# A residual stack in four layers: each step from layer to layer done by token halves

## The reference

```
layer 0: h = rms_norm(x); proj = h @ even_w_in (1024 -> 5120)
         stick-breaking attention (8 heads of 128), a diagonal state-space mixer with GLU
         x = x + concat(o_a, o_b) @ even_w_out            (1536 -> 1024)
layer 1: h = rms_norm(x); proj = h @ odd_w_in (1024 -> 3088)
         gated linear attention (4 heads, chunks of 64)
         x = x + (o * silu(z)) @ odd_w_out                (1024 -> 1024)
layers 2, 3: mod = silu(c) @ w_ada + b_ada -> shift, scale, gate
         h = rmsnorm(x, norm_w) * (1 + scale) + shift
         qa ka va za qr kr vr zr ga gr = h @ w_in         (1024 -> 11264)
         dilated window attention on qa ka va, retention on qr kr vr
         merged = sigmoid(ga) * (y_att @ w_proj_attn) + sigmoid(gr) * (y_ret @ w_proj_ret)
         x = x + gate * (merged @ w_out)
output:  rmsnorm(x, final_norm_w)
```

## Time and profile before

| | us |
|---|---|
| median of 3 runs | 1103.94 |
| the profiled execution, its own time | 1104.06 |
| its span | 1101.1 |
| TensorE busy | 1027.7 (93%) |
| VectorE busy | 706.2 (64%) |
| ScalarE busy | 554.3 (50%) |
| GpSimd busy | 319.2 (29%) |
| TensorE's share of the chain that ended last | 84% |
| VectorE's share of that chain | 9% |

### The profile page before, as it was taken

How to read it: one execution, slowest core, us unless ns; L and a number is a source line. 1 busy time by engine, 2 the same in 40 slices (tenths; PEclk the granted TensorE clock), 3 DMA queues, 4 the chain that set the end, 5 groups by cost and what they waited for, 6 DMA issues and landing times.

```text
span 1101.1 us, 15234 instructions
## 1 busy us (share of the span) xinstructions
PE 1027.7 (93%) x6032; PEld 901.5 (82%) x6032; DVE 706.2 (64%) x1043; ACT 554.3 (50%) x822; POOL 319.2 (29%) x342
## 2 busy tenths in 40 slices
PE   5899999978998799999999989969999999999994
PEld 5688888767976699888899868858998888988883
DVE  6884857568759664556566686676454565758664
ACT  6978577447334354455443334434444555334442
POOL 3600150016323534371708750045150000420001
PEclk9899999989999899999999999989999999999997
DMA  7543424467745676774667655546676436654541
GB/s 236 167 117 100 149 77 145 145 187 253 230 141 179 211 218 205 231 218 141 194 190 220 194 180 174 190 134 205 188 232 188 135 115 176 189 151 148 181 152 57
DMA packets 94470, 191.10 MB, mean 174 GB/s; under 512 B 6800, under 2 KB 10128, under 8 KB 94400
## 3 DMA queue, kind: packets, MB, share of 16 engines
q1 hardware_dynamic: 86256, 164.71, 48.9%
q0 software_dynamic: 6992, 22.72, 6.8%
q10 hardware_dynamic: 1152, 2.71, 0.7%
HBM read 189.07 MB, written 1.05 MB: 173 GB/s over the span
## 4 chain that ended last, share of the span: by engine, by line
PE 84%; DVE 9%; ACT 4%; issue 1%; DMA 1%; DVEq 0%; SPq 0%; ACTq 0%
PE G L579 15%; PE G L581 15%; PE G L580 15%; PE G L588 8%; PE G L590 8%; PE G L591 8%; DVE WL L1494 2%; PE B L542 2%; ACT AR L1039 1%; ACT WH L1039 1%; PE B L675 1%; DVE AR L1594 1%; PE G L615 1%; PE G L614 1%; PE G L613 1%
## 5 line engine op out<-in xcount | busy, mean ns | idle before, releaser
L1494 DVE TENSOR_TENSOR WL<-RAW,WH 128x1024 fp32r<-128x1024 f32 (+2 forms) x306 | 393.9, 1289 | 292.0 <-ACT WH L1039 291.1
L1039 ACT ACTIVATE WH<-RAW 128x1024 fp32r<-128x1024 f32 (+2 forms) x306 | 320.4, 1049 | 297.0 <-PE G L581 168.5
L579 PE MATMUL G<-WH,HTh 128*128 128x512 f32 (+2 forms) x624 | 252.1, 404 | 8.6 <-DVE WL L1494 8.4
L581 PE MATMUL G<-WL,HTh 128*128 128x512 f32 (+2 forms) x624 | 241.5, 387 | 0.0
L580 PE MATMUL G<-WH,HTl 128*128 128x512 f32 (+2 forms) x624 | 241.3, 387 | 0.0
L588 PE MATMUL G<-HTh,WH 128*128 128x256 f32 x736 | 211.4, 287 | 4.9 <-DVE HTl L1599 4.1
L590 PE MATMUL G<-HTl,WH 128*128 128x256 f32 x736 | 208.9, 284 | 0.0
L591 PE MATMUL G<-HTh,WL 128*128 128x256 f32 x736 | 208.8, 284 | 0.0
L588 PEld LDWEIGHTS G<-HTh,WH 128*128 128x128 f32 x736 | 141.9, 193 | 8.3 <-issue 6.9
L579 PEld LDWEIGHTS G<-WH,HTh 128*128 128x128 f32 x624 | 118.4, 190 | 33.8 <-DVE WL L1494 11.1
L590 PEld LDWEIGHTS G<-HTl,WH 128*128 128x128 f32 x736 | 141.9, 193 | 0.6 <-issue 0.5
(11 more groups left out here) (346 smaller groups left out, 1240.2 us busy)
## 6 DMA issues: line engine op xcount, KB each, us to landing
RAW<-in_w_in SPq DMA_DIRECT2D x176, 512.0 KB, 3.8
RAW<-in_even_w_in SPq DMA_DIRECT2D x40, 512.0 KB, 3.6
AR<-in_w_ada POOLq DMA_DIRECT2D x80, 256.0 KB, 3.5
RAW<-in_odd_w_in SPq DMA_DIRECT2D x16, 512.0 KB, 4.5
RAW<-in_w_proj_ret SPq DMA_DIRECT2D x16, 512.0 KB, 3.4
RAW<-in_w_out SPq DMA_DIRECT2D x16, 512.0 KB, 3.5
RAW<-in_even_w_out SPq DMA_DIRECT2D x12, 512.0 KB, 3.5
AR<-in_w_ada SPq DMA_DIRECT2D x16, 256.0 KB, 4.3
```

What stands on the lines that cost most here:

```text
L579: nc.tensor.matmul(o, xh, wh, start=begins, stop=False)
L581: ins = nc.tensor.matmul(o, xh, wl, start=False, stop=ends)
L1039: return nc.scalar.activation(out_, ps, ACT.Copy, **kw)
L1494: vt(wl, raw, wh.bitcast(F32), ALU.subtract).then_inc(*dve.mark(LO, n))
```

## The change

Every step from layer to layer is now done first for tokens 0-127 and then for tokens 128-255:

- The last three pieces of a layer are of kind C, instead of the last two: column half 0 with the last rows, column half 1 with the rows before the last, column half 1 with the last rows. All three run for tile 0, then all three for tile 1 (`split_half`).
- The first three pieces of layers 1, 2 and 3 are done the same way (`opening`): three half steps for tile 0, three for tile 1. They are of kind N, which a split needs; in layers 2 and 3 the `va` groups therefore move ahead of `qa` and `ka`.
- `rstd`, `scaled`, `square` and `turned` work on one tile each. VectorE scales columns 0-511 of a tile and GpSimd columns 512-1023 (before: VectorE and ScalarE). The turned blocks are evicted in runs of 128x128; in layers 2 and 3 ScalarE applies shift and scale (before: VectorE).
- `hi` of the new layer's first piece moves behind the first squares; the tables of ScalarE and VectorE end 6 half steps before a layer's end instead of 4.
- HN32 now lies on OR. GpSimd's modulation tasks of layers 2 and 3 each wait for a piece to be read (`pool.wait_ge(*read(time // 2 - 1))`) and have new places in the table. At the start of layer 1 three DMAs of GpSimd stand behind its two scalings.
- The first norm (layer 0) is also done by tiles on VectorE and GpSimd, and its transposes in the order column half 0 for both tiles, column half 1 for both.

The first `next_layer` below is ScalarE's, the second VectorE's, and `scaled` is GpSimd's:

```diff
-AT_ADA1 = tuple(2 + 30 * g + 3 * k + (36 if g > 5 else 0) for g in range(8) for k in range(8))
+AT_ADA1 = tuple(8 + 29 * g + 3 * k + (0, 20, 50)[g // 2 - 1 if g > 3 else 0] for g in range(8) for k in range(8))
...
+        def closing(l, w, ks, lhs, into):
+            v = w.rearrange("(c p) n -> p c n", p=P)
+            groups["close", l] = dict(into=into, at=len(pieces), n=512)
+            for j, k in ((0, ks[1]), (1, ks[0]), (1, ks[1])):
...
+        def opening(name):
+            for i in range(3):
+                pieces[groups[name]["at"] + i]["split"] = i
...
-                if p["kind"] == "C":
-                    closing_half(n, kk, p)
+                if p["split"] is not None:
+                    h = 2 * p["split"] + kk
+                    split_half(n - p["split"] + h % 3, h // 3)
...
+            def open_layer(l, first):
+                for q in range(2):
+                    norm_turn(l, 0, q)
+                for i in range(6):
+                    half(first + i)
+                    if i in (1, 2):
+                        norm_turn(l, 1, i - 1)
...
+            def next_layer(l):
+                square(l - 1, 0, 0)
+                square(l - 1, 0, 1)
+                hi(n0)
+                square(l - 1, 1, 0)
+                hi(n0 + 1)
+                turned(l, 0, 0)
+                square(l - 1, 1, 1)
+                turned(l, 0, 1)
+                hi(n0 + 2)
+                turned(l, 0, 2)
+                turned(l, 0, 3)
+                for r in range(4):
+                    turned(l, 1, r)
...
+            def next_layer(l):
+                residual(l - 1, 0, 0)
+                residual(l - 1, 0, 1)
+                residual(l - 1, 1, 0)
+                rstd(l, 0)
+                scaled(l, 0)
+                residual(l - 1, 1, 1)
+                lo(n0)
+                turned(l, 0, 0)
+                turned(l, 0, 1)
+                lo(n0 + 1)
+                rstd(l, 1)
+                scaled(l, 1)
+                lo(n0 + 2)
+                turned(l, 0, 2)
+                turned(l, 0, 3)
+                for r in range(4):
+                    turned(l, 1, r)
...
+            def scaled(l, ti):
+                pool.wait_ge(*RSTD.of(l, ti))
+                gts(HN[:, ti, 512:1024], X[:, ti, 512:1024], NR[l][:, ti:ti + 1], 0.0, ALU.mult, ALU.add).then_inc(
+                    *pool.mark(HN_P, l, ti))
...
             for l in range(2):
-                norm(2 + l)
+                next_layer(2 + l)
                 ts(GNH[l], co[f"gn{l}"], 0.5, None, ALU.mult).then_inc(*dve.mark(GNH_V, l))
...
+                        pool.wait_ge(*read(time // 2 - 1))
```

More of the change, by code:

```diff
@@ L1033, in gbank @@
             return G[groups[name]["into"][ti]]
-        ENDS = {2 * last_of(n) + 1: n for n in groups if n[0] not in ("o0c", "close")}
+        ENDS = {2 * last_of(n) + 1: n for n in groups if n != "o0c" and n[0] != "close"}
         def scalar_program():
@@ L1350, in scalar_program @@
             nc.scalar.activation(er, er, ACT.Exp).then_inc(*act.mark(S5_A, "er"))
-            for time in range(2 * groups["zr"]["at"] - 4):
+            for time in range(2 * groups["zr"]["at"] - 6):
                 if time in ENDS:
@@ L1400, in scalar_program @@
                     hi((time + 1) // 2 + AHEAD)
-            for ti in range(2):
-                squares(0, ti)
-            norm(1)
-            for time in range(2 * groups["zr"]["at"], 2 * H0[0] - 4):
+            next_layer(1)
+            for time in range(2 * groups["zr"]["at"], 2 * H0[0] - 6):
                 if time in ENDS:
@@ L2096, in residual @@
-            def residual(l):
-                for ti in range(2):
-                    dve.wait_ge(*tile(("close", l), ti))
-                    for n in range(2):
-                        ps = G[groups[("o0a", "o0b")[n] if l == 0 else ("o1", n)]["into"][ti]]
-                        x = X[:, ti, 512 * n:512 * n + 512]
-                        vt(x, ps[:, :], x, ALU.add).then_inc(*dve.mark(RES_V, l, ti, n))
-            nc.vector.memset(M3[:, :, :, :].rearrange("p a b c -> p (a b c)"), 0.0).then_inc(*dve.mark(S5_V, "zero"))
@@ L2164, in vector_program @@
                     lo((time + 1) // 2 + AHEAD)
-            residual(0)
-            norm(1)
+            next_layer(1)
             ts(go, co["gla_o_g"], 0.5, None, ALU.mult).then_inc(*dve.mark(GO, "g"))
-            for time in range(2 * groups["zr"]["at"], 2 * H0[0] - 4):
+            for time in range(2 * groups["zr"]["at"], 2 * H0[0] - 6):
                 if time in ENDS:
@@ L2366, in pool_program @@
             nc.gpsimd.memset(flat(NEAR), 0.0).then_inc(*pool.mark(S5_P, "near"))
[L2368 removed]
+            for ti in range(2):
+                scaled(0, ti)
+            for time in range(2 * groups["zr"]["at"] - 6):
                 if time == AT_S5["powers"]:
@@ L2378, in pool_program @@
             ada_load(0, 0)
-            pool.wait_ge(*read(53))
+            for ti in range(2):
+                scaled(1, ti)
             nc.gpsimd.dma_start(GM, const("glamask")).then_inc(l_gm, 16)
```

375 lines of the change are left out of this document (186 added, 189 removed).

## The result

The changed kernel took 1093.45 us (median of four runs, 1090.39 to 1093.97) against 1103.01 for the kernel before in the same comparison (four runs): ratio 0.991, 95% interval 0.988 to 0.994. That is 9.6 us faster, inside the forecast range and 1.7 us under the forecast. The profiled execution took 1093.02, its span 1091.2. The two profiled executions lie 11.0 us apart, their spans 9.9; the other 1.1 is outside the spans (2.96 us before, 1.8 after) and is not the change, since most later executions of the kernel before have 1.8 to 2.0 there too.

The account below looks back on a forecast made before the run. TensorE, busy 93% of the span, was taken as the bound, gaining only where it stands or runs slowly. Terms -0.6 - 4.7 - 7.4 - 1.6 + 2.3 + 3.1 = -8.9 gave 1095.2, median 1095.1 us; range 1089.5 to 1101.5.

Parts of the forecast that it names:

- The chains between the layers: From each layer's last matmul to the next layer's fourth piece: 0.6, 4.7 and 7.4 us gained at the three boundaries.
- T: End of a layer's last closing matmul (its start plus 0.39 us), from which the prediction counts times.
- Layer 1 to 2: Boundary between these layers: fourth piece at T+17.2 instead of T+21.87, 4.7 us gained.
- Layer 2 to 3: Boundary between these layers: fourth piece at T+18.35 instead of T+25.75, 7.4 us gained.
- the 1.0 that I put on tile 0's root beside GpSimd's add: Layer 2 to 3: GpSimd's add for tile 1 holds the port, so tile 0's rsqrt ends 1.0 us later.
- The end: Behind the last matmul: 2.1 us of work and waiting falls away, final weights' DMA takes 0.5 back, 1.6 gained.
- The start: Program's start: rsqrt chains one behind the other, VectorE waiting for GpSimd's memset, first matmul at 18.5, 2.3 us lost.
- The clock in the openings: Openings of layers 1 to 3: half steps two to four at 1.2 GHz, 3.1 us lost together.
- The GpSimd rival: Modulation tasks hold the port through layer 2's attention and retention; six more tasks lose 12 us, result 1107; chance 0.06.
- the four places of the change: The three layer boundaries and the program's end: gains of 0.6, 4.7, 7.4 and 1.6 us.
- losses of 5.4: Losses in the sum: 2.3 us at the program's start and 3.1 for TensorE's low clock in the openings.

Follow-up runs that it names:

- Closing whole: Changed kernel with each layer's last three pieces multiplied piece by piece, both token halves within each, instead of all three for tokens 0-127 first: 1102.1 us, ratio 0.998.
- scale_first: Changed kernel with GpSimd's clearing of buffers at the start put behind its scaling of tile 0 (the 128x2048 one behind both tiles): 1093.06 us, ratio 0.9915.
- mod_early: Changed kernel with the fifth group of GpSimd's eight modulation tasks 20 steps earlier in layer 2, out of the retention: 1090.6 us, ratio 0.9875.
- mod_around: Changed kernel with layer 2's fifth group of modulation tasks laid around the retention, four before and four after, the sixth group at steps 182-203: 1090.52 us, ratio 0.9887.
- fw_early: Changed kernel with the final norm's weights loaded in layer 3 and the first final product ahead of tile 1's reciprocal root: 1090.48 us, ratio 0.9884.
- order_only: Kernel before with only the piece order in layers 2 and 3 changed, attention's values first, then queries and keys: 1104.21 us, ratio 1.0001.

## Why the prediction was right, and where it was not

- **The chains between the layers: right in kind; in the sizes two errors cancelled.** Forecast fourth pieces T+14.75, T+17.2, T+18.35; measured T+14.35, T+18.10, T+18.46. First half step of layer 2 T+3.0, measured T+3.3. Transposes in groups of 8, 4, 4 with a first gap of 0.7, as forecast. Undoing either split showed that it is this chain and no side effect; how much of the split opening's part is the clock is not separated.
  - *Layer 1 to 2, 0.9 too much.* VectorE was on time: its scaling of tile 1 ended at T+8.6 for T+8.5. But GpSimd's, counted at 0.70, took 2.04 beside VectorE's `lo`, and VectorE's eviction behind the `lo` took 0.83 where 0.42 was counted, and where all others of its kind here measure 0.41 to 0.43; it ended 0.27 behind GpSimd's scaling:

```profile
376.55 2.04 POOL L2363 TENSOR_SCALAR TK<-X,SM 128x512 f32<-128x512 f32 x1 [7.00 <-DVE SM L1598]
```

```profile
378.02 0.83 DVE L1618 TENSOR_TENSOR HTl<-AR,HTh 128x256 fp32r<-128x256 f32 x1
```

  TensorE's third half step waited for that eviction and came at T+10.66 for T+10.1; everything of tile 1 stands behind it. GpSimd's columns themselves were not waited for: their transposes ran at 380.46, 1.9 us after its scaling. The other 0.3 is small excess behind the last eviction (T+15.6 for T+15.0): the group-norm instruction and a `lo` of 1.23.
  - *Layer 2 to 3, right by luck.* It has the same 0.9, and yet came only 0.1 late, since the 1.0 that I put on tile 0's root beside GpSimd's add was too much. The add ran from T-1.9 to T-0.6, and of the root's instructions beside it one took 0.47 instead of 0.22; VectorE's scaling ended 0.36 later than in layer 1 to 2, not 1.0, and the fourth piece came those 0.36 later, T+18.46 for T+18.10.
- **The end: near in size, on the wrong path.** 2.2 for 1.6. I followed VectorE's last product, and it ends at T+8.5 for T+9.4 before, 0.9 earlier and not 1.6. The span's end comes 7.6 us behind GpSimd's last product in every profile, and that one moved by 2.2, from T+8.85 to T+6.64: it no longer stands behind the root of both tiles, only behind the final weights. Closing whole confirms it: GpSimd's product ends at T+9.34 there, 2.7 later, as does the span.
- **The start: the step that failed.** I had the first tiny instruction of tile 0's root wait for GpSimd's clearing, since it took 2.42 us before. After:

```profile
6.08 0.15 DVE L1579 TENSOR_SCALAR SM<-SM 128x1 f32<-128x1 f32 x1 [0.94 <-ACT AR L1387]
...
8.07 2.59 DVE L1603 TENSOR_SCALAR TK<-X,SM 128x512 f32<-128x512 f32 x1
```

  The whole root ran beside the clearing, at 0.15 to 0.22 us an instruction; only the 128x512 scaling waited. The first matmul came at 16.17, not 18.5, and the term of 2.3 us measured 0.0 at T of layer 0. The instruction that waited before was 128x2, one column for each tile; now it is 128x1. The Trainium skill (VectorE: DVE Perf Modes, "Mode 2×_2P — use both read ports for one tensor") gives both read ports to a one-source operation from SBUF to SBUF whose outermost non-unit dimension is even, or odd and equal in source and destination, and (SBUF — State Buffer, "Who interferes with whom") has such an operation blocked by GpSimd. By that rule 128x2 and 128x512 wait; 128x1, which has no such dimension, doesn't. The traces agree in all three: 2.42, 2.59 and 0.15 us. No run here has the old 128x2 root in the new order, so the width as the cause rests on these rows and the rule. And `scale_first` showed that even a start 2.3 us earlier is worth nothing.
- **The clock in the openings: the term was of the wrong kind.** It stayed at 1.00 from 1 to 2 and fell at 0 to 1 and 2 to 3, but in the half steps that wait for VectorE anyway. The fourth piece of 2 to 3 came at T+18.46 with the clock at 0.60 in 732 to 736, and at T+18.49 in `mod_early` with no fall there. Where the fall reaches the dense half steps of tile 1 it costs about 1 us: T+15.37 for T+14.35 in `mod_around`, T+19.0 for T+18.1 in `mod_around` and `fw_early`. The 3.1 should have been 0 to 1 for each boundary, by where the fall lies, and in the forecast's sum it measured 0.
- **Inside the layers: a rival in part.** The GpSimd rival (tasks that hold VectorE up in the retention) was priced at 12 us for six more tasks; I had named it and then put nothing into the sum. What came is 2.6 us in layer 2, and it isn't more waiting: the longest wait grew from 2.05 to 3.38, but all waits of TensorE over 0.25 us behind the fourth piece sum to 4.5 before, 4.2 after and 3.0 in `mod_early`. What differs is the clock behind the wait, 0.50 from 649.9 to 656.7 and 1.00 throughout before. Moving the tasks took 2.4 us away in the profile, half of it waits. The +1.1 in layer 1 is not the change: the same 2.50 us wait stands in both kernels, and the clock behind it stayed up in the profile before and fell in the one after. `order_only`, whose layer 1 is the one of before, has the fall too. The stretches 268 to 272 of before, after and `order_only`:

```profile
268.00:272.00 4.00, 1.50 (x7) 0.96 (x6) 3.97 (x4) 2.49 (x3) 3.40 (x3) 1.00 0.57 179
```

```profile
268.00:272.00 4.00, 1.50 (x5) 0.95 (x4) 4.00 (x4) 2.89 (x4) 3.32 (x4) 0.88 0.46 148
```

```profile
268.00:272.00 4.00, 2.26 (x5) 1.84 (x6) 4.00 (x4) 2.95 (x3) 3.77 (x3) 0.66 0.48 136
```

So 1095.1 for 1093.45 was close for two reasons: the four places of the change were right to 0.1 us in sum, with errors of -0.4, +0.9, +0.1 and -0.6 us that cancel, and losses of 5.4 at the wrong places stood for 4.4 at others. The mechanism was foreseen; so near a number is luck. What decides whether the clock falls behind a given wait stays open. The +0.6 in layer 3 is the new order: `order_only` has 0.5 of it with nothing else changed. 0.4 of that would be three pieces of kind T now behind the fourth instead of three of kind N, at 0.14 each.

## What to carry to other kernels

Where a norm stands between two layers, split both the last work of one and the first work of the next by the same rows: here either split alone left 2 to 3 us of the 10, and work by tiles without them lost 10.7 against the kernel before. Write the chain out from the last bank of the first half, every engine's queue in order, and look for small instructions with a wait on the wrong side of it (0.17 us of work held 0.67 twice). At the end of a program, look at which engine the end follows: here it was GpSimd's last product and not VectorE's. Background work on GpSimd is then the next lever: eight tasks placed away from VectorE's gates gave as much in the total (2.9 us) as the best single edit behind the splits (3.0, `fw_early`), though neither interval is clear of the changed kernel's.

## What the hardware showed that was not expected

- Beside VectorE's `lo` (two inputs in SBUF), GpSimd's 128x512 scaling took 2.04 us for 0.97, the `lo` kept its 1.2, and VectorE's next two-input instruction took 0.83 for 0.42.
- GpSimd's memsets let VectorE's 128x1 operations through at 0.15 us, and held a 128x512 one for 2.59 (0.48 alone). Being small is no protection beside a product of GpSimd, though: in `fw_early` a 128x1 instruction with two inputs, 0.22 us otherwise, took 1.16, to within 0.01 us of the product's end (1079.95 to 1081.21):

```profile
1080.06 1.16 DVE L1594 SCALAR_TENSOR_TENSOR SM<-SM 128x1 f32<-128x1 f32 x1
```

- Sixteen idle transposes in the gaps did not keep the granted clock up; they moved two of its falls by 5.7 us, to where they cost more, and a third did not come.
- One kernel's executions differ by where the clock falls: `scale_first` ran 1091.8 to 1093.4 five times, and 1099.82 once, with the clock at 0.50 from 68 to 80 under a TensorE that was busy throughout.
